# TensorE's order in the mixer loop: the attention output product in larger pieces, intermediate products ahead of the second head's values, states ahead of the third's

## What is computed

```python
y_a = band attention (4 heads, own 64-row chunk and 8 before, bias on the distance)
y_b = mLSTM           # num = inter * q @ c + wqk @ v ; c = decay * c + (ws * k)^T @ v
y_c = Mamba-2 SSD     # y = (cb * dec * dt) @ x + exp(cs) * c @ h ; h = exp(cs) * h + (wl * x)^T @ b
y_d = gMLP gate
mix = concat([y_a, y_b, y_c, y_d]) @ w_out
x   = x + gt1 * mix
h2  = rmsnorm(x, g_ffn) * (1 + sc2) + sh2
```

## Time and profile before

| | before |
|---|---|
| timed runs, us | 3173.46, 3177.63, 3180.89 (median 3177.63) |
| profiled execution, us | 3168.1, span 3166.4 |
| mean granted TensorE clock | 0.95 of full |
| TensorE busy | 2846.8 us, 90% of the span |
| TensorE loading weights | 2548.5 us, 80% |
| VectorE, ScalarE, GpSimd busy | 41%, 31%, 8% |
| the mixer loop | about 988 to 1510 us, a late tile 30.9 us |

### The profile page before, as it was taken

The page is one execution under the profiler, slowest core; times in us unless marked ns, Lnnn a source line. Parts: engine busy times, 40 slices in busy tenths (PEclk is TensorE's granted clock), DMA queues, the critical chain, the costliest instruction groups (busy, mean ns, idle before and its releaser), DMA issues.

```text
span 3166.4 us, 41936 instructions
## 1 busy us (share of the span) xinstructions
PE 2846.8 (90%) x16292; PEld 2548.5 (80%) x16292; DVE 1297.1 (41%) x2483; ACT 982.1 (31%) x1682; POOL 245.0 (8%) x413
## 2 busy tenths in 40 slices
PE   4499999999272999999599999999999999999987
PEld 1288888999252788887599998789999878999975
DVE  2333334342142554554233334544433454544444
ACT  1133334332131444444222223332222333222333
POOL 0000000000021432332000000000000000000000
PEclk8699999999685999999699999999999999999998
DMA  9622324211517444342522224433222443322344
GB/s 296 213 72 93 109 71 153 89 67 70 166 15 201 152 140 126 125 129 71 138 61 66 60 66 141 158 109 104 64 62 66 135 156 113 114 73 74 99 130 145
DMA packets 342266, 355.48 MB, mean 112 GB/s; under 512 B 44423, under 2 KB 283659, under 8 KB 341684
## 3 DMA queue, kind: packets, MB, share of 16 engines
q1 hardware_dynamic: 326738, 349.02, 35.4%
q10 hardware_dynamic: 15396, 4.66, 0.8%
HBM read 285.75 MB, written 70.10 MB: 112 GB/s over the span
## 4 chain that ended last, share of the span: by engine, by line
PE 46%; DVE 2%; DMA 2%; SPq 1%; issue 1%; ACT 0%; POOL 0%; DVEq 0%; ACTq 0%
PE acc_ps L2873 14%; PE acc_ps L2829 11%; PE acc_ps L2830 11%; PE acc_ps L2831 11%; DMA w_raw<-in_f_w_down 1%; DMA xr<-scratch_x 0%; DVE y L3121 0%; SPq L2773 0%; DVE w_lo L3095 0%; DMA out_y_prompt<-y 0%; ACT w_hi L2968 0%; DVE xr L3115 0%; DMA ffn_gate_in<-scratch_ffn_gate 0%; DVE prod L3109 0%; DVE w_lo L3038 0%
## 5 line engine op out<-in xcount | busy, mean ns | idle before, releaser
L2829 PE MATMUL acc_ps<-h_hi,w_hi 128*128 128x384 f32 (+1 forms) x2112 | 690.3, 327 | 6.3 <-DVE w_lo L3038 6.1
L2830 PE MATMUL acc_ps<-h_lo,w_hi 128*128 128x384 f32 (+1 forms) x2112 | 689.5, 326 | 0.0
L2831 PE MATMUL acc_ps<-h_hi,w_lo 128*128 128x384 f32 (+1 forms) x2112 | 689.5, 326 | 0.0
L3038 DVE TENSOR_TENSOR w_lo<-w_raw,w_hi 128x1024 fp32r<-128x1024 f32 x242 | 296.5, 1225 | 662.7 <-ACT w_hi L2926 652.9
L2926 ACT ACTIVATE w_hi<-w_raw 128x1024 fp32r<-128x1024 f32 x242 | 256.6, 1060 | 800.5 <-PE acc_ps L2831 524.0
L2829 PEld LDWEIGHTS acc_ps<-h_hi,w_hi 128*128 128x128 f32 x2112 | 397.9, 188 | 7.8 <-DVE w_lo L3038 6.5
L2830 PEld LDWEIGHTS acc_ps<-h_lo,w_hi 128*128 128x128 f32 x2112 | 397.9, 188 | 0.1
L2831 PEld LDWEIGHTS acc_ps<-h_hi,w_lo 128*128 128x128 f32 x2112 | 397.8, 188 | 0.0
L2873 PE MATMUL acc_ps<-w_hi,mid_hi 128*128 128x512 f32 x748 | 236.1, 397 | 30.3 <-DVE mid_lo L3099 15.8
L2873 PE MATMUL acc_ps<-w_hi,mid_lo 128*128 128x512 f32 x748 | 233.2, 393 | 0.0
L2873 PE MATMUL acc_ps<-w_lo,mid_hi 128*128 128x512 f32 x748 | 233.0, 393 | 0.0
(11 more groups left out here) (490 smaller groups left out, 4155.7 us busy)
## 6 DMA issues: line engine op xcount, KB each, us to landing
w_raw<-in_f_w_down SPq DMA_DIRECT2D x122, 512.0 KB, 3.5
w_raw<-in_f_w_gate SPq DMA_DIRECT2D x66, 512.0 KB, 3.9
w_raw<-in_f_w_up SPq DMA_DIRECT2D x66, 512.0 KB, 3.9
w_ada<-in_w_ada SPq DMA_DIRECT2D x12, 2048.0 KB
m_bc<-scratch_bc SPq DMA_DIRECT2D x16, 768.0 KB, 5.1
scratch_tok<-p_m SPq DMA_DIRECT2D x17, 640.0 KB, 2.9
m_tok<-scratch_tok SPq DMA_DIRECT2D x16, 640.0 KB, 4.8
scratch_ht<-p_m SPq DMA_DIRECT2D x17, 512.0 KB, 3.3
```

The source lines that it names most:

```text
L2829: t.matmul(dst, hi, h2_hi[:, k, cols], start=(k == 0), stop=False)
L2830: t.matmul(dst, hi, h2_lo[:, k, cols], start=False, stop=False)
L2831: last = t.matmul(dst, lo, h2_hi[:, k, cols], start=False, stop=(k == KD - 1))
L3038: v.tensor_tensor(w_lo[j][:], raw[j][:], w_hi[j][:], ALU.subtract).then_inc(s_lo[j], 1)
```

## The change

TensorE's calls in a step are the same, in another order. The output product's first half is done in pieces of four and four k-blocks, where it was three, two and three. `turn_h2(q, 0)` comes ahead of `attend(i, 0)`, `nums` and `ys` ahead of `attend(i, 1)`, `states` ahead of `attend(i, 2)`. No other engine's program is touched.

```diff
--- before.py
+++ after.py
@@ -2244,35 +2244,32 @@
                 if on:
                     qk(i)
                 if o is not None:
-                    out_part(o, 0, range(0, 3))
+                    out_part(o, 0, range(0, 4))
                 if on:
                     turn_probs(i, 0)
+                if q is not None:
+                    turn_h2(q, 0)
                 if o is not None:
-                    out_part(o, 0, range(3, 5))
+                    out_part(o, 0, range(4, 8))
                 if on:
                     attend(i, 0)
-                if q is not None:
-                    turn_h2(q, 0)
-                if on:
                     scores(i, 1)
                     turn_probs(i, 1)
                 if q is not None:
                     turn_h2(q, 1)
-                if o is not None:
-                    out_part(o, 0, range(5, 8))
                 if on:
-                    attend(i, 1)
                     nums(i)
                     ys(i)
+                    attend(i, 1)
                 if o is not None:
                     out_part(o, 1, range(0, 4))
                 if on:
                     turn_probs(i, 2)
+                    states(i)
                 if o is not None:
                     out_part(o, 1, range(4, 6))
                 if on:
                     attend(i, 2)
-                    states(i)
                     turn_probs(i, 3)
                 if o is not None:
                     out_part(o, 1, range(6, 8))
```

## The result

| | before | after |
|---|---|---|
| timed runs, us | 3173.46 to 3183.51, median 3179.26 | 3236.12 to 3247.03, median 3238.43 |
| profiled execution, us | 3168.1, span 3166.4 | 3238.45, span 3236.7 |
| mean granted TensorE clock | 0.95 | 0.933 |
| first to last record of L2053 (from the start of tile 0 to the start of tile 15, give or take 0.4 us) | 987.7 to 1456.2, 468.5 us | 987.2 to 1512.4, 525.2 us |

The changed kernel is slower by 1.92% (ratio 1.0192, 95% interval 1.0167 to 1.0217), some 59 us where 13 were forecast. The difference lies in the mixer loop: 525.2 - 468.5 = 56.7 us.

What follows compares the result with a forecast made beforehand. TensorE's queue was taken to bound the mixer stage. New wait 13.2, earlier states -0.9 and joins +1.0 gave +13.3 us, put to the runs' median 3177.63: 3190.9 us, 0.42% slower, range 3181 to 3198.

Steps and rivals of the forecast that it cites:

- The wait: At `nums`, TensorE waits for VectorE's reading of all four heads' scores: 0.75 us in 12 tiles, 13.2 us in all.
- `qk`'s 10.1 us: At `qk`, TensorE's wait behind VectorE's `make_gt`, 10.1 us in 14 tiles, was to stay as before.
- VectorE's wait of L2559 for the states: Before `next_states`, VectorE's 0.72 us wait was to go, buying no time in a late tile.
- the 0.9 forecast: In the first tiles, earlier `states` was to shorten the wait at L2100 behind `finish_a`: -0.9 us.
- The joins: Where TensorE switches between transposes and matmuls: 0.06 us a tile more, +1.0 us in all; high end 0.15 a tile, 2.4 us.
- a join is free: At output product pieces, a slower first matmul (0.32 against 0.23 us) is offset by shorter preceding transposes; one less saves nothing.
- rival (c): In the mixer loop, the clock falls, 12 product matmuls running low in each of 16 tiles: 38 us more, 3229; 2%.
- Rival (a): At the tile's end, earlier `states` carries through to `make_gt` and `qk`'s wait vanishes: -10.0 us, 3167.6; 4%.
- Rival (d): At `turn_h2(q, 0)`, a wait arises if ScalarE is 1.8 us later: some 0.5 us a tile more, 3199; 3%.

Runs made afterwards that it cites:

- Experiments 5 and 6: The changed kernel with seven (5) or three (6) more transposes in `turn_h2(q, 1)`, in the place of the wait of `nums`: 3192.64 us and 3193.13 us.
- experiment 9: The changed kernel with `make_gt` and `yt_low(o, 0)` ahead of `largest(i, 1)` and `yt_high(o, 0)` ahead of `probs(i, 0)`: 3217.54 us, ratio 1.0145.

## Why the prediction was wrong

- **The wait was right.** The place (L2198 behind `largest`), the count (16) and the one large one in tile 1 (2.3 us against 2.36) came as worked out; 12.1 us were recorded against 13.2, 0.69 a tile for 0.75. The 0.69 is the idle time that the row records; from the start of `turn_h2(q, 1)` to the start of `nums` are 1.29 us (1420.66 to 1421.95), and the forecast had 0.54 + 0.75. `qk`'s 10.1 us stayed, VectorE's wait of L2559 for the states is gone, and `states` ahead brought 0.7 us at L2100 for the 0.9 forecast. Experiments 5 and 6 show the time with the clock held in the late tiles: 17 and 18 us over the kernel before, where I had 13.3. Part of that is the low stretch in tile 1, which they keep.
- **The joins were undersized.** I took 0.06 us a tile, with 0.15 as the high end. The changed kernel's undisturbed tile is 0.92 us longer; by the forecast's own split, with 0.75 for the wait, 0.17 are joins, and by the recorded 0.69 they are 0.23. That is 2.7 to 3.7 us instead of 1.0. The fault lay in "a join is free". A piece's first matmul takes 0.09 us more wherever the piece begins; only transposes ahead of it give that back, since the step from them to a product is as much shorter (0.46 for five). Of the six pieces before, four had transposes ahead, of the five now only two: the others follow `qk`, `attend(i, 1)` and `states` (1184.76 to 1185.08, 0.32 again). So three pieces pay where two did, +0.09, beside the +0.10 that the forecast had for one more step from transposes to fp32 matmuls: 0.19, an estimate from these rows, for the 0.17 measured.
- **The step that failed is rival (c), in its weight.** The forecast put the clock's cost at nothing. The mechanism of (c) is what happened, and it got 2%. Its price (38 us) was near the 43 measured, and that was luck in part: it let 12 product matmuls run low in each of 16 tiles, where ten of the twelve late tiles and two early ones had 6.8 or 10.2 us of it, mostly `ys`, `attend(i, 1)` and the first products. The reason given against it compared "the run of transposes, scores and the wait from L2053 to `qk`", 4.7 us, with a new one of "0.60 + 0.54 + 0.75 us". The two were cut by different rules. Counted alike, from one matmul of the output product to the next, the old run is 6.6 us and the new one 10.1, which the order of the change shows without any trace: `attend`, scores, transposes, `nums`, `ys` and `attend` in a row. The longest such stretch grew by half and got a standstill into its middle, and the loop before had nothing of that length at the full clock to vouch for it. With the right comparison this was an open case, and the range had to reach it.
- The rule quoted with it, from the Trainium skill ("TensorE: Matmul & The Clock Gate", Part 4: PE-mode transpose), that transposes don't count as busy for the clock gate, is not what experiments 5 and 6 show: fp32 transposes in the place of 0.69 or 0.33 us of standstill, between other matmuls, brought the clock back to 1.00 in the late tiles with nothing else changed.
- Rival (a), the gain at the seam, was rightly small: moving `states` left `qk`'s wait at 10.1 us. Rival (d) did not occur; L2187's only wait is the 5.0 us after the last tile that the kernel before has too.

What stays open: the rule by which the clock falls. In these kernels it fell in most late tiles only where two things came together, a stretch of some 10 us without the 512-column products and a standstill of 0.69 us in it. With the standstill in a stretch of 7.2 or 9.0 us it fell in two and in four of eleven, with the long stretch and no standstill or half of it in none. They don't show why two of the changed kernel's late tiles (31.82 and 31.83 us long) escaped and the nine after them did not, or why experiment 9 falls every third tile. Nor was it tried what it takes at other lengths.

## What to carry to other kernels

When an order is changed on the engine that bounds the kernel, add up the waits, and then measure the longest stretch between its densest matmuls before and after: if it grows, the granted clock is at risk. Here 12.1 us of waits inside such stretches brought some 43 us of clock with them. Put such a wait, if there must be one, next to dense work, or fill it; here even work that is thrown away paid. And when an engine's wait is removed by moving one producer up, look at what the next instruction waits for: here the same 10 us stood 0.7 us further on until two engines' orders were changed together.

## What the hardware showed that I had not expected

- With a standstill of 0.69 us in each tile of 31.8 us the clock halved for 6.8 or 10.2 us in nine late tiles out of eleven, and with one of 0.36 us at the same place in none.
- Busy time did not show the slow stretches: at the low level the records of matmuls cover all of the time (10.20 of 10.20 us), and at the full one they do too but for the two standstills (25.87 of 27.30).
- Filling the wait cost nothing: tiles with seven more transposes, with three, and without any (undisturbed) are all 31.82 to 31.85 us long.
